# The first layer's mixer in another order: modulation pieces among the projection units, group A of stream 1 between the steps of stream 0's group C

## The reference

```python
mod = (jax.nn.silu(cvec) @ ada_w[l] + ada_b[l])[:, None, :]
sh1, sc1, g1, sh2, sc2, g2 = jnp.split(mod, 6, axis=-1)
o, new = token_mixer(rms_norm(x, norm1_g[l]) * (1 + sc1) + sh1, lw, ctx)
x = x + g1 * o
x = x + g2 * channel(rms_norm(x, norm2_g[l]) * (1 + sc2) + sh2, l)
```

## Time and profile before

| | |
|---|---|
| median of 3 runs | 1634.72 us (1633.57 to 1637.39) |
| the profiled execution | 1634.51 us, span 1632.9 us |
| granted TensorE clock, mean | 0.964 |
| PE busy | 1533.8 us (94%) |
| DVE busy | 1173.0 us (72%) |
| ACT busy | 914.4 us (56%) |
| DMA | 523.26 MB, mean 320 GB/s |
| chain that ended last | PE 82%, DVE 8%, ACT 4%, DMA 3%, issue 2% |

### The profile page before, as it was taken

One profiled execution on the slowest core, in us unless ns is written; L12 is line 12 of the kernel. 1 busy time (PEld: TensorE's weight loads), 2 busy tenths in 40 slices (PEclk: granted clock), 3 DMA queues, 4 the chain that ended last, 5 costly groups with the idle time before them and its releaser, 6 DMA issues.

```text
span 1632.9 us, 19705 instructions
## 1 busy us (share of the span) xinstructions
PE 1533.8 (94%) x7058; PEld 1179.3 (72%) x7058; DVE 1173.0 (72%) x1215; ACT 914.4 (56%) x789; POOL 66.5 (4%) x105
## 2 busy tenths in 40 slices
PE   6888879999998777999999999999999999999997
PEld 3555447888656544888888888888888888888885
DVE  1364564445436354688889888888889888889988
ACT  1213234344231313577877877877877777777774
POOL 1500000000001000100000000000000000000200
PEclk9998999999998698899999999999999999999999
DMA  9969978865686266699999999999999999999992
GB/s 355 325 204 413 338 239 268 266 204 199 235 284 190 106 233 232 235 397 369 378 380 367 391 388 370 383 375 376 392 363 385 387 363 386 379 377 370 396 403 117
DMA packets 192569, 523.26 MB, mean 320 GB/s; under 512 B 10624, under 2 KB 71200, under 8 KB 187400
## 3 DMA queue, kind: packets, MB, share of 16 engines
q1 hardware_dynamic: 167440, 493.39, 82.0%
q0 software_dynamic: 6768, 18.63, 3.3%
q10 hardware_dynamic: 18312, 10.60, 2.1%
HBM read 505.49 MB, written 17.08 MB: 320 GB/s over the span
## 4 chain that ended last, share of the span: by engine, by line
PE 82%; DVE 8%; ACT 4%; DMA 3%; issue 2%; SPq 0%; ACTq 0%; DVEq 0%
PE PS L601 21%; PE PS L603 21%; PE PS L602 21%; PE PS L716 5%; PE PS L607 5%; DMA ring<-in_ada_w 2%; PE PS L931 2%; PE PS L682 2%; DVE parts L2033 1%; PE PS L746 1%; PE PS L730 1%; ACT parts L1431 1%; PE PS L621 1%; ACT arena L1274 1%; DMA ring<-in_w_in 1%
## 5 line engine op out<-in xcount | busy, mean ns | idle before, releaser
L2033 DVE TENSOR_TENSOR parts<-ring,parts 128x2048 fp32r<-128x2048 f32 x336 | 766.3, 2291 | 109.2 <-ACT parts L1431 107.0
L1431 ACT ACTIVATE parts<-ring 128x2048 fp32r<-128x2048 f32 x336 | 643.9, 1919 | 216.6 <-PE PS L603 216.5
L601 PE MATMUL PS<-parts 128*128 128x512 f32 x1608 | 633.5, 394 | 8.1 <-DVE parts L1678 4.1
L603 PE MATMUL PS<-parts 128*128 128x512 f32 x1608 | 627.8, 390 | 0.0
L602 PE MATMUL PS<-parts 128*128 128x512 f32 x1608 | 627.5, 390 | 0.0
L601 PEld LDWEIGHTS PS<-parts 128*128 128x128 f32 x1608 | 302.6, 188 | 74.0 <-DVE parts L2033 7.1
L603 PEld LDWEIGHTS PS<-parts 128*128 128x128 f32 x1608 | 302.4, 188 | 64.2
L602 PEld LDWEIGHTS PS<-parts 128*128 128x128 f32 x1608 | 302.7, 188 | 61.9 <-issue 0.2
L1592 DVE TENSOR_TENSOR parts<-ring,parts 128x2048 fp32r<-128x2048 f32 x33 | 75.5, 2289 | 52.8 <-PE PS L603 50.0
L716 PE MATMUL PS<-ring,xnT 128*128 128x420 f32 (+1 forms) x240 | 91.7, 532 | 0.0
L1215 ACT ACTIVATE parts<-ring 128x2048 fp32r<-128x2048 f32 x33 | 63.0, 1916 | 29.6 <-PE PS L603 29.6
(11 more groups left out here) (310 smaller groups left out, 932.0 us busy)
## 6 DMA issues: line engine op xcount, KB each, us to landing
ring<-in_moe_w SPq DMA_DIRECT2D x336, 1024.0 KB, 6.9
ring<-in_ada_w SPq DMA_DIRECT2D x40, 1024.0 KB, 8.5
ring<-in_w_in SPq DMA_DIRECT2D x32, 840.0 KB, 11.6
ring<-in_ffn_w SPq DMA_DIRECT2D x44, 512.0 KB, 5.0
ring<-in_w_out SPq DMA_DIRECT2D x16, 1024.0 KB, 7.8
ring<-in_ffn_w SPq DMA_DIRECT2D x11, 1024.0 KB, 4.8
expert_rows<-zeros ACTq DMA_DIRECT2D x17, 512.0 KB, 4.2
ring<-in_ada_w SPq DMA_DIRECT2D x16, 512.0 KB, 11.3
```

What stands on the lines that cost most here:

```text
L601: mm(out, s_hi, m_hi, start=start, stop=False)
L603: return mm(out, s_lo, m_hi, start=False, stop=stop)
L1431: A(w_hi(j), slot(n), ACT.Copy).then_inc(hi_ready, 1)
L2033: TT(w_lo(j, 3), slot(W0 + j), w_hi(j).bitcast(f32), ALU.subtract).then_inc(split_done, 1)
```

## The change

Only two lines of the tables change, both of the first layer.

```diff
--- before.py
+++ after.py
@@ -37,12 +37,12 @@
 
 
 PHASE_1 = {0: """
-A0 i1 A0 i1 A0 i1 A0 B0 i1 B0 i1 n1 B0 i1 i1 B0 B0 t0 i1 C0 t0 i1 C0 t0 i1 C0 a a a a a C0 g1 a C0 a a C0 a C0
+A0 i1 A0 i1 A0 i1 a A0 B0 i1 a B0 i1 n1 a B0 i1 a B0 B0 t0 a i1 C0 a t0 t0 i1 C0 a i1 C0 a a i1 A1 A1 C0 g1 C0 l1 c1 A1 C0 A1 C0
 """, 1: """
 A0 i1 A0 i1 A0 i1 A0 B0 i1 B0 i1 n1 B0 i1 B0 B0 t0 i1 C0 t0 t0 i1 C0 i1 C0 i1 A1 A1 C0 g1 C0 l1 c1 A1 C0 A1 C0
 """}
 PHASE_2 = {0: """
-A1 l1 a A1 a c1 a a A1 a A1 B1 a B1 a B1 a o0 o0 B1 B1 a C1 t1 a C1 t1 t1 a C1 o0 a o0 a a C1 a C1 a a o0 C1 r0 r0 a C1
+a a B1 a a B1 a B1 a a a o0 o0 B1 B1 a C1 a t1 C1 t1 t1 a C1 o0 a a o0 a C1 a C1 a a o0 C1 r0 r0 a C1
 """, 1: """
 a B1 a B1 a B1 o0 o0 B1 B1 a C1 t1 C1 t1 t1 a C1 o0 a o0 C1 a C1 a o0 C1 r0 r0 a C1
 """}
```

## The result

| | median, us | lowest to highest | runs |
|---|---|---|---|
| before | 1635.53 | 1633.57 to 1637.39 | 4 |
| changed | 1652.66 | 1649.67 to 1654.30 | 4 |

The changed kernel takes 1.0103 times as long, 95% interval 1.0081 to 1.0124: slower by 17.1 us. The direction was forecast, the size was not: 1646.5 was predicted, with 1651.5 as the upper end. Its profiled execution took 1654.17 us (span 1652.6, mean granted clock 0.956).

A forecast was written before the change was run, and what follows sets the result against it. TensorE, busy in 94% of the span, was taken as the bound. E +15.5, E to S -5.8 and +2.3 behind S sum to +12.0 on 1634.5: 1646.5 us; its own range 1642 to 1651.5, overall 1636.5 to 1651.5.

The forecast's parts named there:

- Step 3: Before the transposes behind the eighth piece: TensorE waits 5.3 us for DVE's L1602, behind L1897; bounds 4.5 to 6.
- S: Mark: start of stream 1's group B (L791), at 153.8 us before, forecast near 163.5.
- the two signs of a wrong forecast: A wait before the transposes under 3 us, or S before 158 us.
- Step 5: From E to S: groups alternate, two pieces follow; 39.0 us become 33.2, so -5.8; bound above -5.0.
- E: Mark: end of the last projection unit, at 114.8 us before, forecast 130.3.
- Step 4: Last projection unit, right behind the new wait: the granted clock falls, 0 to +2.9 us, +1.3 taken.
- Step 2: Stream 0's group B: four pieces less a unit would be +1.0 us, forecast +0.8, so the term is -0.2.
- step 6: Inside stream 1's group B: three pieces more, partly filling TensorE's wait before L931; +2.3 us, 1.5 to 3.9.
- the shift behind R: Behind R: same operations, later two swaps of neighbours; nothing there taken as gain or loss.
- R: Mark: first output projection matmul (L931), at 165.15 us before, forecast near 177.
- The clock stays high: Rival: no low clock in the alternating stretch and at the last unit; +2.8 us, 1637.3; chance 0.20.
- Landings replace the DVE wait: Rival: stores delay loads, last unit's weights land up to 2 us behind the transposes; 1648.0 us; chance 0.05.

The follow-up runs named there:

- norms behind: Changed kernel with the eighth piece and the transposes ahead of the third step (norms) of stream 0's group C: 1646.43 us, ratio 1.0050.
- the alternation alone: Kernel before with nine pieces in a row behind the last unit, then the changed order, groups A and C alternating: 1653.70 us, ratio 1.0102.
- the larger set of dummies: Kernel before with unread matmuls in the second layer's alternation, plus fifteen more, mostly late in that layer: 1617.83 us, ratio 0.9898.

## Why the prediction was right and wrong

**Right: the wait and its cause.** Step 3 gave 5.3 us behind L1897, 4.84 came, put down to L1602 as named. L1602 ended at 127.5 by the marks of before (129.8 less 2.3), 2.4 us later than the forecast 125.1. Two ways of taking it away gained 6.2 and 8.5 us. S stands at 166.7 and the wait is over 3 us, so neither of the two signs of a wrong forecast appeared, and the landings stayed behind. Step 5 was on the safe side: E to S took 32.1 us and not 33.2.

**Wrong: low clock outside steps 4 and 5 was put at nothing.** Step 4's own term was large enough: the unit took 0.9 us more than at full clock, where 1.3 was taken. What failed are steps 2, 3 and 6 and the shift behind R. Low clock was priced for the transposes, for this unit and, in the 29.5 us and its two pieces, for step 5; steps 2, 3 and 6 took their pieces and units at full clock or at that of before, and the shift behind R was put at nothing. The sum missed 5.3 us of the profiled 17.3. From A0 to the end of stream 0's L877 the shift was 5.4 instead of 2.8 us (from L834 on at 0.81 instead of 0.88, L834 itself 3.68 us instead of 2.36). S to R took 4.07 us more instead of 2.3, over step 6's own bound of 3.9 (0.78 instead of 0.85). R to dense took 2.7 us more instead of nothing (0.93 instead of 0.97). Together these are 7.1 us over the sum; 0.6 came back around the wait and the unit, and 1.2 in step 5. In the whole mixer the clock stood at 0.5 for 23.9 us more than before.

How the clock's part divides over the stages can't be read from one profile each. Up to L877 two of the experiments have the changed order too, and reach its end 50.3 us behind A0, not 52.4 (norms behind; transposes behind the last unit). Behind R the kernel with the alternation alone has the changed order and took 66.1 us to dense, not 69.0, while the kernel with dummies in the second layer alone is the kernel before in this layer and took 69.0 where the profile of before shows 66.35. So the 2.7 us behind R are within what identical code scatters by. The total is firmer: the four executions lie within 4.6 us of each other, all with a clock below before's medians, and eleven dummies took back thirteen microseconds.

Two smaller slips stand in the working. Step 2 has three pieces more ahead of L827, where four stand; TensorE came there at 97.3 us by the marks of before, not at 95.2, and didn't wait for L1794. And the upper end's +18.1 for E is 18.4 by its own terms (eight pieces at 1.07, 1.1, -0.2, 6 and 2.9). Neither would have brought the forecast to 17 us.

**The rule that I weighed.** The Trainium skill, page "TensorE: Matmul & The Clock Gate", section "Terms", prices throttled time at one minus the clock ratio. For 23.9 us more at 0.5 that gives an estimate of 12.0; the trace agrees, with 11.3 us more busy time. I had set it against one stretch only. My own model had the same limit: the second layer's 29.5 us had that stretch's low clock built in, and I didn't ask what the clock would do in the stretches around it.

**The rivals.** "The clock stays high" was priced at 1637.3. The experiment that comes nearest to it, eleven dummies in the waits, took 1639.4, with 25.8 us from E to S where that case has 26.05. So the price of that case was about right; what was at fault is the other side, as my upper bound had the second layer's clock for the alternation and hardly a worse one elsewhere. "Landings replace the DVE wait" didn't occur in the changed kernel (0.24 us). It did when the transposes were moved (2.02 us).

**Where the expected gain went.** The saving was to be the landings' 5.7 us and the 2.6 us for exponentials. Moving three pieces at either place shows that these waits lay inside latency of ScalarE and DVE that pieces were covering. Taken from there, the same latency stands bare: 5.62 us at L1897 and 4.30 at L1277. The changed kernel's 4.84, 4.75 and 2.19 I read in the same way. What stays open is how the clock's part divides over the stages, and why removing the 4.84 us by moving the transposes gained 8.5 us and removing it by moving the norms 6.2: their ranges overlap, and the two kernels ran on different chips.

## What to carry to other kernels

A wait for a load may lie inside the latency of another engine, and then removing it gains nothing. Before moving filler work away from such a place, look for the run of ScalarE and DVE that ends there, and ask what will cover it. Price a new order by the granted clock of every stretch that it touches, those behind included, with the low time of the whole stage and not of one stretch. Where waits of 1 to 6 us can't be removed, matmuls that nothing reads, few enough to end before what is waited for, can keep the clock up: they gave back 13.2 of 17.1 us here, and made the kernel before 1.0% faster. At the landings' waits of up to 1.4 us they gained nothing. A kernel so treated has a higher clock than the one that it is compared with, so equal times don't mean that the order costs nothing.

## What the runs showed of the hardware

- **The clock's falls differ between executions of the same code.** In the first layer's mixer the kernel before and the one with dummies in the second layer alone are the same, and the clock fell in different places behind R (66.35 and 69.0 us to dense). The kernel with the larger set of dummies is the kernel before up to stream 1's group C, and S lies at 88.7 and 88.8 us from A0 in the two profiles, but then S to R took 14.0 us there and 11.3 in before, with the clock at 0.5 from 147.3 to 161.0. One kernel's executions spread over 1616.5 to 1627.8 us, another's over 1639.7 to 1654.1. With 10 to 12 executions of a kernel, differences of 0.2 to 0.3% came out clear of their intervals.
- **For 9 us behind stream 0's stores the DMA moved little.** POOL issued stream 0's stores at 103.3 to 105.2 us of the kernel before, and SP the next load at 105.66; between 101 and 104.4 nothing was under way. The GB/s moved from 100 to 135 us, in 40 slices of 0.875 us:

```profile
GB/s 56 0 0 0 0 150 3 159 9 19 84 37 37 28 66 66 290 412 431 431 431 421 403 440 440 431 412 431 412 412 431 412 440 431 403 403 440 431 421 421
```

  and issues of 100 to 110 us (the last row: of 120 to 130): out<-in, queue, operation, count, KB each, median us to landing:

```profile
ring<-in_ada_w SPq DMA_DIRECT2D x2, 1024.0 KB, 10.8
out_new_mlstm_C<-arena POOLq DMA_DIRECT2D x1, 128.0 KB, 2.8
out_new_mla_ckv<-ckv_out POOLq DMA_DIRECT2D x1, 64.0 KB, 8.2
out_new_mlstm_n<-arena POOLq DMA_DIRECT2D x1, 2.0 KB, 6.3
...
ring<-in_ada_w SPq DMA_DIRECT2D x4, 1024.0 KB, 17.5
```

  From the stores to 114 us the rate stays far under the later 400 and more: 60 GB/s from 104.4 to 114.0, with the DMA engines busy for a share of 0.75, and 418 at 1.01 from 114 to 135. The store of 2 KB took 6.3 us to land, more than 128 KB with 2.8. The loads' own landing times don't show the slow stretch: the two asked for right behind the stores took 10.8 us, the six of the earlier trace rows 14.3, and the four asked for at 120 to 130 us, at the full rate, 17.5. Landing times so long at the full rate fit more loads under way at once. That too is an inference, as is that the stores hold the loads back, which reads the order in time as a cause. Neither was tried.
